# Gated linear attention: the place of the output copy and of the backward state update in the chunk loop

## The reference, cut to what matters

```
def gla_scan(q, k, v, log_a, S0):
    def step(S, inp):
        qx, kx, vx, ax = inp
        b = jnp.cumsum(ax, axis=1)
        diff = b[:, :, None] - b[:, None, :]
        decay = jnp.where(causal, jnp.exp(jnp.minimum(diff, 0.0)), 0.0)
        scores = jnp.einsum('bthc,bshc,btshc->btsh', qx, kx, decay)
        o = jnp.einsum('btsh,bshe->bthe', scores, vx) + jnp.einsum('bthc,bhce->bthe', qx * jnp.exp(b), S)
        b_last = b[:, -1]
        S_new = jnp.exp(b_last)[..., None] * S + jnp.einsum('bshc,bshe->bhce', kx * jnp.exp(b_last[:, None] - b), vx)
        return S_new, o
```

## Time and profile before

| | us |
|---|---|
| median of 3 runs | 3271.03 |
| lowest and highest of them | 3269.95, 3274.26 |
| the profiled execution: its own time | 3268.45 |
| the profiled execution: its span | 3266.7 |
| median above the profiled execution's time | 2.58 |

### The profile page before, as it was taken

One profiled execution on the slowest core, in us unless ns is written; L12 is line 12 of the kernel. 1 busy time (PEld: TensorE's weight loads), 2 busy tenths in 40 slices (PEclk: granted clock), 3 DMA queues, 4 the chain that ended last, 5 costly groups with the idle time before them and its releaser, 6 DMA issues.

```text
span 3266.7 us, 44403 instructions
## 1 busy us (share of the span) xinstructions
PE 2998.5 (92%) x17516; PEld 2617.0 (80%) x17516; DVE 2137.6 (65%) x2709; ACT 1217.9 (37%) x1938; POOL 1281.0 (39%) x851
## 2 busy tenths in 40 slices
PE   7999868999889999999999999857879999999998
PEld 3898657899768999978877898646768999978876
DVE  3688679555477744478887555477777744478886
ACT  2311133555454322333323476543344322233322
POOL 1211046100022543478871211145443544478870
PEclk9999989999889999999999999966689999999999
DMA  5476544100032233233351332321132233233341
GB/s 206 157 258 204 190 143 122 48 13 1 11 104 84 80 103 110 78 133 107 110 167 53 128 130 74 124 89 49 33 106 85 80 103 110 77 132 109 110 168 58
DMA packets 230815, 347.01 MB, mean 106 GB/s; under 512 B 32040, under 2 KB 124240, under 8 KB 230608
## 3 DMA queue, kind: packets, MB, share of 16 engines
q1 hardware_dynamic: 230608, 344.17, 31.6%
HBM read 259.18 MB, written 84.94 MB: 105 GB/s over the span
## 4 chain that ended last, share of the span: by engine, by line
PE 66%; POOL 12%; DVE 11%; issue 5%; ACT 3%; DMA 2%; SPq 1%; POOLq 0%; DVEq 0%; ACTq 0%
PE psum L979 18%; PE psum L1171 8%; PE psum L656 8%; POOL d_slot L1111 6%; PE psum L2454 4%; PE psum L659 4%; PE psum L1276 3%; PE psum L1624 3%; PE psum L2442 2%; PE psum L2449 2%; PE psum L2754 2%; PE psum L1153 2%; DVE mix_x L2937 1%; PE psum L426 1%; DVE mix_v L2950 1%
## 5 line engine op out<-in xcount | busy, mean ns | idle before, releaser
L1171 PE MATMUL psum<-d_slot 128*128 128x512 f32 x2016 | 465.0, 390 | 11.8 <-DVE yacc L1216 6.9
L1171 PEld LDWEIGHTS psum<-d_slot 128*128 128x128 f32 x2016 | 377.3, 188 | 95.4 <-DVE yacc L1216 8.6
L979 PE MATMUL psum<-AT,w_slot 128*128 128x288 f32 x2688 | 366.0, 295 | 4.8 <-POOL w_slot L944 4.8
L979 PEld LDWEIGHTS psum<-AT,w_slot 128*128 128x128 f32 x2688 | 359.5, 188 | 5.2 <-POOL w_slot L944 5.2
L1111 POOL TENSOR_TENSOR d_slot<-down_a,d_slot 128x512 fp32r<-128x512 f32 x168 | 300.1, 1810 | 72.2 <-ACT d_slot L1102 72.0
L591 POOL TENSOR_TENSOR WT<-RAW,WT 128x1024 fp32r<-128x1024 f32 (+3 forms) x34 | 115.2, 3413 | 457.3 <-ACT WT L580 457.3
L656 PE MATMUL psum<-WT,AT 128*128 128x512 f32 (+1 forms) x1296 | 280.6, 377 | 4.1 <-ACT stage L702 4.1
L979 PE MATMUL psum<-s_hi,w_slot 128*128 128x288 f32 x1344 | 269.1, 295 | 5.9 <-issue 4.3
L656 PEld LDWEIGHTS psum<-WT,AT 128*128 128x128 f32 x1296 | 230.6, 189 | 47.0 <-ACT stage L702 4.3
L944 POOL TENSOR_TENSOR w_slot<-RAW,w_slot 128x512 fp32r<-128x512 f32 x112 | 155.8, 1402 | 224.2 <-ACT w_slot L940 224.2
L979 PEld LDWEIGHTS psum<-s_hi,w_slot 128*128 128x128 f32 x1344 | 215.2, 188 | 7.1 <-issue 5.2
(11 more groups left out here) (431 smaller groups left out, 6083.6 us busy)
## 6 DMA issues: line engine op xcount, KB each, us to landing
RAW<-ffn_w SPq DMA_DIRECT2D x40, 1024.0 KB, 6.5
ada_raw<-ada_w SPq DMA_DIRECT2D x36, 1024.0 KB, 6.4
hidden<-hid SPq DMA_DIRECT2D x56, 576.0 KB, 3.3
down_a<-hidden SPq DMA_DIRECT2D x48, 512.0 KB, 6.4
RAW<-ffn_w SPq DMA_DIRECT2D x48, 512.0 KB, 8.1
RAW<-w_in_even SPq DMA_DIRECT2D x5, 2048.0 KB, 8.0
RAW<-w_in_odd SPq DMA_DIRECT2D x5, 2048.0 KB, 7.8
mix_x<-x_all SPq DMA_DIRECT2D x18, 512.0 KB, 3.6
```

Source lines behind the costliest of these rows:

```text
L979: mm = nc.tensor.matmul(psum[:, bank + b, 0:HB], w_slot[p][:, w, k, :], TOKENS[p][x][:, k, b * HB:(b + 1) * HB], start=(begins and k == 0 ...
L1171: mm = nc.tensor.matmul(psum[:, D_RING[q % 3] + pair % 2, :], slot[:, 0, x, k, pair * P:(pair + 1) * P], slot[:, 1, w, k, :], start=(k == ...
```

## The change

Three edits in the chunk loop.

1. ACT: `keep_o(v - 1)` leaves step 3 and stands in step 6, behind the exponential of level 6.
2. DVE: `new_state(v - 1, 1)` and `backward_out(v - 1)` stand in step 0 of pass v, behind `factors(v, 2)` and in front of `put(v, 0)`. `new_state(v - 1, 0)`, with the clearing of the state in pass 8, stands behind the `put` of step 5 and no longer behind that of step 6. `add_o` and the remainder stay behind the `put` of step 7.
3. DVE: `factors(v, 2)` no longer waits for level 0 of its own tile, which doesn't read gl_F, only for level 6 of the tile before.

```
                     if step == 3:
-                        if v and o_is_first(v - 1):
-                            keep_o(v - 1)
                         state_exp(v, 0, 0)
                         state_exp(v, 0, 1)
...
+                    if step == 6 and v and o_is_first(v - 1):
+                        keep_o(v - 1)
                     if step == 7:
                         keep_kT(v)
...
-                dve.wait_ge(wi_mm[p], per_step(v, step))
+                dve.wait_ge(wi_mm[p], per_step(v, step) - (step == 2))
...
-                if step == 4:
+                if step == 0:
                     new_state(v, 1)
+                    backward_out(v)
                 elif step == 5:
                     new_state(v, 0)
...
-                    backward_out(v)
...
-                    if step == 6 and v:
-                        behind(v - 1, 4)
+                    if step == 0 and v:
+                        behind(v - 1, 0)
                     put(v, step)
-                    if step in (6, 7) and v:
-                        behind(v - 1, step - 1)
+                    if step in (5, 7) and v:
+                        behind(v - 1, (step + 5) // 2)
                 if v + 1 < TILES:
                     first_factors(v + 1)
-            for step in range(4, 7):
+            for step in (0, 5, 6):
                 behind(TILES - 1, step)
```

## The result

The changed kernel takes 3239.22 us (median of 4 runs, 3236.03 to 3242.9) against 3270.49 for the kernel before (4 runs beside it); the ratio is 0.9906 with a 95% interval of 0.9888 to 0.9924. Two later sets of runs gave 0.9910 (0.9895 to 0.9925) and 0.9908 (0.9895 to 0.9922). So it is faster by about 30 us. The forecast was 20.8 us faster, 3250.2, with a range from 3241 to 3261: the direction is right, and the time lies just outside the range.

What follows compares the result with a forecast made beforehand. The chunk loop was taken as bound by waits: POOL for ACT, ACT for `out`, PE for `new_state` and `backward_out(7)`. Gains 10.4 + 9.5 + 0.9 = 20.8 us off 3271.03 gave 3250.2, range 3241 to 3261.

Steps and rivals of the forecast that it cites:

- The copy, 10.4 us: ACT's keep_o to step 6: the first four periods fall from 25.37 to 22.76 us; 10.4 us gained, bounds 5 and 12.
- it would meet DVE (0.10): Rival: POOL released sooner runs beside DVE and slows it, so passes 1 to 4 keep half of their 2.61 us; 3255.4, chance 0.10.
- The update in front of the transposes, 9.5 us: Backward state update leaves step 6, so PE's wait in front of the transposes goes: 8 x 1.19 = 9.5 us gained.
- Its new place, 0: Update and backward_out in step 0, in front of put(v, 0): put done at 9.4 us, before level 2 asks; costs 0.
- The rival that the update gives its gain back (0.10): In step 0 the update holds up put(v, 0), level 2 waits, and the 9.5 us are lost; 3259.7, chance 0.10.
- the cover of 2.0 us: Slack in step 0, walked through from pass 6 to 7: put of level 0 ends 2.0 us before level 2 needs it.
- The relaxed wait, 0 by itself: DVE's factors(v, 2) moves in front of level 0: gains 0 by itself but frees the place in step 0.
- Pass 8, 0.9 us: In pass 8, from_state's wait for backward_out(7) goes: 0.9 us gained, bounds 0 and 0.9.
- The granted clock, 0 with 2 us either way: PE's clock rise behind the transposes: no change counted, between a gain and a loss of 2 us over nine passes.
- The prediction's own sign of being wrong: One of three stated signs: the clock in the stretches behind the transposes rises elsewhere.
- The rival of a clock that rises sooner (0.05, 3236.7): Without the pause, TensorE's clock rises up to 3 us sooner in nine passes, 13.5 us more gained; 3236.7, chance 0.05.
- The slower rival (0.02): The clock's stretch at the high level is lost, costing 5.6 us a pass, 50 in nine; 3300, chance 0.02.

Runs made afterwards that it cites:

- The last kernel: Changed kernel plus 6, 4 and 4 unread matmuls behind levels 2, 3 and 4, and DVE's four remainders made behind the last pass: 3212.79 us, ratio 0.9841.

## Why the prediction was wrong, step by step

*What bounds the kernel.* Right. The waits that it named are the ones that went.

*The copy, 10.4 us.* Right in its waits. Alone it gave 14.6 us (10 to 20 by the interval), and the late periods of that run, 22.7 to 22.9, are the 22.76 that the step took from the last four. The excess is the early periods'. POOL's wait became 4.1 us and not 5.3, since the pause of 1.2 us between its last exponents and the transposes is gone too. That it would meet DVE (0.10) and cost half of this shows nowhere: the first periods had 21.40 and 21.50 us.

*The update in front of the transposes, 9.5 us.* Right. The first two periods of the changed kernel, 21.40 and 21.50, stand 0.1 us under the 22.76 - 1.19 = 21.57 that was forecast. With the copy left in step 3 the other number is 23.8 to 23.9, where taking the pause off gave 23.5.

*Its new place, 0.* Right: `put` ended at 9.0 us against 9.4 in the walk. The rival that the update gives its gain back (0.10) didn't come true. But the cover of 2.0 us was worked out in a pass without DVE's remainder. Behind pass 4, which carries one, it was 0.4 us; where the clock was also up, in the runs with extra matmuls, PE waited up to 2.36 us.

*The relaxed wait, 0 by itself.* Right, and needed by the rest: without it 6.5 us of new waits were measured, where the walk had about 5 (0.6 to 0.7 a pass).

*Pass 8, 0.9 us.* Right: the wait is gone. The end of the stage gained 2.4 us, and the other 1.5 are the clock again: it rose 3.8 us sooner, and the rows of `into_state` and `from_state` above are shorter by just that.

*The granted clock, 0 with 2 us either way.* This is the step that failed. It stood on one row, the rise of pass 0, and on the sentence that its place drifts. Six periods of the changed kernel were 20.34 to 20.76 us and not 21.45, the mean of the first two: that is 6 x 0.95 = 5.7 us. With pass 8 (1.5) the clock brought 7.2 us where the sum had 0. The periods of both kinds also stand 0.12 under the forecast's 21.57, which is 8 x 0.12 = 1.0 us more. That is all of the 29.0 - 20.8 = 8.2 us that the stage gained beyond the forecast; with it the forecast would have been 3242.0. The rest, 3.4 us of the profiled execution, is outside the stage and within what runs of one kernel differ. The prediction's own sign of being wrong, a clock that rises elsewhere behind the transposes, came true.

The row that it stood on was of the pass least like the others: in pass 0 of the kernel before, PE had waited 3.28 us in front of level 2 and 1.22 in front of level 6. The trace of before had better evidence. In its pass 1 (transposes at 2191.82) the clock was up from 2197.5, and it was still at its upper level in this stretch, over 9 us later, where each other pass had it for under 7.

```profile
2205.00:2207.00 2.00, 0.83 (x16) 1.00 0.14 51
```

A reader of the clock of all nine passes, and not of one, would have found both kinds of pass, and a first price: 24.79 us for the period with the long stretch, 25.69 and 26.03 for its neighbours. It isn't a clean one, since pass 3, with an early rise and a short stretch, had 24.97; the 1.1 us come from the run with the copy alone. And such a reader would have asked where a shorter period takes the rise.

*The rival of a clock that rises sooner (0.05, 3236.7)* came nearest in time, and its sign was right, but the mechanism that it gave isn't the cause: the missing pause is neither needed for the early rise nor enough for it. The rival wanted the missing pause to bring the rise forward. With the pause back the early rise still came in every second pass, and with no pause but 0.5 us more work it came in two of eight. The slower rival (0.02) had the clock's part with the wrong sign. The Trainium skill (TensorE: Matmul & The Clock Gate, "What's actually happening") names sustained activity as what releases the throttle. The last kernel agrees, with the clock up throughout, but the rule doesn't say in which pass of this loop the rise is early.

What stays open: why the rise keeps its place at 5.3 to 5.8 us once it is there in the changed kernel. The runs show that it settles with a period of 20.2 to 20.8 us in three profiles of it, that it alternates at a mean period of 22.2 and that it stays at 7.8 us with 23.88. A rise whose place isn't tied to the pass would explain all of these. The profiles speak for it: in the run with the copy alone and in the one with the pause back, a rise follows the one before by 20.5 and 23.9 us in turn, with no value between, while the passes are 21.4 to 22.9 us long. A loop of about 20.5 or of 23.9 us then keeps the rise in place, and one of 22.2 doesn't. In that reading the missing pause helped after all, by making the pass shorter. No run has tested it apart from the period. The long stretch also didn't follow every early rise: in the run without the relaxed wait, a rise at 5.4 us was followed by a short one, and in the kernel before one at 5.9.

## What to carry to other kernels

Where TensorE alternates between its two clock levels inside a loop, read the rise and the fall in every pass before pricing an edit: where the rise fell early in a pass and the upper level then lasted 10 us and not 7, it was worth another 1.1 us, as much as the wait that was taken away. Work out the cover of moved work in the pass that has the least of it, and for the clock at its upper level too: 1.6 us behind one pass were 0.4 behind another here. And where PE waits in short gaps that let its clock fall, a few matmuls that nobody reads can be worth more than the next wait: here they and the move of 5.4 us of DVE work together brought 22 us.

## What the runs showed of the hardware that wasn't expected

Twelve matmuls of 128 by 128 that cost 2.94 us with the clock up cost 5.29 with it down, so the same filler that held the clock made the pass slower where it failed to. And the clock stayed at its upper level through 145 us of this stage with PE busy for 43.69 of 45 and 94.83 of 100 us, while in the changed kernel, whose middle levels left gaps of 0.6 to 1.8 us, it fell in every pass.
